# A mixture of 16 experts in two layers: experts written out, tile slots in strict turn, combination products moved, constants issued by SyncE

## The reference

```python
def expert_choice_ffn(h, w_router, w_gate, w_up, w_down):
    b, n, d = h.shape
    cap = max(1, (EC_CAPACITY * n) // N_EXPERTS)
    aff = jax.nn.softmax((h @ w_router).astype(jnp.float32), axis=-1)
    g, idx = lax.top_k(jnp.swapaxes(aff, 1, 2), cap)
    xe = jax.vmap(lambda hb, ib: hb[ib])(h, idx)
    a = jnp.einsum('becd,edf->becf', xe, w_gate)
    up = jnp.einsum('becd,edf->becf', xe, w_up)
    y = jnp.einsum('becf,efd->becd', jax.nn.silu(a) * up, w_down) * g[..., None].astype(h.dtype)
    return jax.vmap(lambda ib, yb: jnp.zeros((n, d), h.dtype).at[ib.reshape(-1)].add(yb.reshape(-1, d)))(idx, y)
```

## Time and profile before

| what | value |
|---|---|
| median of 3 runs | 2744.36 us (2743.35 to 2745.78) |
| the profiled execution's own time | 2746.78 us |
| its span (first to last instruction) | 2745.0 us |
| PE busy | 2536.9 us, 92% |
| DVE busy | 1403.9 us, 51% |
| ACT busy | 1012.0 us, 37% |
| POOL busy | 32.3 us, 1% |
| DMA, mean over the span | 290 GB/s, 796.95 MB |
| granted TensorE clock, mean | 0.991 |

### The profile page before, as it was taken

One profiled execution on the slowest core, in us unless ns is written; L12 is line 12 of the kernel. 1 busy time (PEld: TensorE's weight loads), 2 busy tenths in 40 slices (PEclk: granted clock), 3 DMA queues, 4 the chain that ended last, 5 costly groups with the idle time before them and its releaser, 6 DMA issues.

```text
span 2745.0 us, 33174 instructions
## 1 busy us (share of the span) xinstructions
PE 2536.9 (92%) x12537; PEld 1678.3 (61%) x12537; DVE 1403.9 (51%) x2437; ACT 1012.0 (37%) x1890; POOL 32.3 (1%) x45
## 2 busy tenths in 40 slices
PE   8999997777899999877789999999999999999999
PEld 5666432222465553322237788877888988887887
DVE  4988200001276530000124788668887468975776
ACT  5224111001121421000004656566565456655544
POOL 0000000000000000000000000000000000000000
PEclk9999999999999999999999999999999999999999
DMA  8767799999965369999994487616866418863242
GB/s 353 316 286 278 332 380 426 427 426 428 426 253 240 154 251 426 427 425 427 427 425 204 179 338 279 250 62 253 328 259 275 184 71 327 312 249 127 95 188 100
DMA packets 65268, 796.95 MB, mean 290 GB/s; under 512 B 9276, under 2 KB 10556, under 8 KB 15484
## 3 DMA queue, kind: packets, MB, share of 16 engines
q1 hardware_dynamic: 61424, 790.65, 70.3%
q10 hardware_dynamic: 3724, 4.66, 0.5%
HBM read 794.23 MB, written 1.05 MB: 290 GB/s over the span
## 4 chain that ended last, share of the span: by engine, by line
PE 70%; DMA 19%; DVE 7%; ACT 2%; issue 2%; SPq 0%; ACTq 0%; DVEq 0%
PE banks L2305 12%; PE banks L2316 9%; PE banks L1682 7%; DMA ring<-in_t_up 6%; DMA ring<-in_t_down 6%; PE banks L994 6%; DMA ring<-in_t_gate 6%; PE banks L1007 5%; PE banks L1702 5%; PE banks L2318 4%; PE banks L1761 3%; PE banks L1904 1%; PE banks L749 1%; PE banks L2028 1%; PE banks L871 1%
## 5 line engine op out<-in xcount | busy, mean ns | idle before, releaser
L1682 PE MATMUL banks<-ring,arena 128*64 128x512 f32 x1904 | 432.4, 600 | 84.5 <-DMA ring<-in_t_gate 45.3
L3054 DVE TENSOR_TENSOR arena<-arena,banks 128x512 f32<-128x512 f32 x32 | 22.0, 687 | 757.2 <-PE banks L1682 757.2
L2316 PE MATMUL banks<-u_pair,w_hi 128*128 128x512 f32 x1024 | 362.8, 399 | 1.7 <-DVE u_pair L1284 1.7
L3601 DVE TENSOR_TENSOR ring_lo<-ring,w_hi 128x1024 fp32r<-128x1024 f32 x256 | 311.8, 1220 | 99.1 <-ACT w_hi L2816 97.3
L1682 PEld LDWEIGHTS banks<-ring,arena 128*64 128x64 f32 x1904 | 138.9, 137 | 364.6 <-issue 263.3
L2816 ACT CAST w_hi<-ring 128x1024 fp32r<-128x1024 f32 x256 | 267.6, 1050 | 197.0 <-PE banks L2305 139.9
L2318 PE MATMUL banks<-u_pair,ring_lo 128*128 128x256 f32 x1024 | 287.6, 281 | 0.0
L2465 ACT COPY arena<-banks 32x512 f32<-32x512 f32 (+1 forms) x96 | 55.3, 576 | 499.1 <-PE banks L1702 498.2
L1702 PE MATMUL banks<-ring,arena 128*64 128x512 f32 x896 | 206.1, 608 | 28.3 <-DVE arena L3056 10.5
L2316 PEld LDWEIGHTS banks<-u_pair,w_hi 128*128 128x128 f32 x1024 | 192.4, 188 | 51.3 <-ACT arena L1254 3.7
L2305 PE MATMUL banks<-w_hi,ffn_h_hi 128*128 128x512 f32 x512 | 199.4, 389 | 0.0
(11 more groups left out here) (420 smaller groups left out, 4162.9 us busy)
## 6 DMA issues: line engine op xcount, KB each, us to landing
ring<-in_t_ffn SPq DMA_DIRECT2D x64, 2048.0 KB, 8.1
ring<-in_t_gate SPq DMA_DIRECT2D x60, 2048.0 KB, 29.4
ring<-in_t_ada_dots SPq DMA_DIRECT2D x54, 2048.0 KB, 9.7
ring<-in_t_down SPq DMA_DIRECT2D x48, 2048.0 KB, 28.6
ring<-in_t_up SPq DMA_DIRECT2D x43, 2048.0 KB, 30.3
ring<-in_t_ada SPq DMA_DIRECT2D x18, 2048.0 KB, 17.1
ring<-in_t_up SPq DMA_DIRECT2D x32, 1024.0 KB, 28.5
ring<-in_t_ret_in SPq DMA_DIRECT2D x12, 2048.0 KB, 8.0
```

Of the source, the lines that this page charges most:

```text
L1682: mm = nc.tensor.matmul(PS[64 * h:64 * h + 64, f.bank, :], x, wview(u, 4)[:, k % 4, h * 512:(h + 1) * 512], start=(k == 0), stop=(k == KC ...
L2316: nc.tensor.matmul(PS[:, f.bank, :], hi[:, q, :], u_pair[:, q].rearrange("p s t -> p (s t)"), start=(q == 0), stop=False, skip_group_check ...
L3601: TT(w_lo, w, w_hi[:, n % 4].bitcast(F32), ALU.subtract).then_inc(S("ffn_w_lo"), 1)
```

## The change

- **Experts written out.** All 16 experts stand in the programs of PE, DVE and SP; ACT keeps its loop. All 96 tiles of a layer are one list, and only the last expert's up and second down tiles are sent in pieces.
- **Strict turn.** Tile n takes slot n mod 7 in layer 0 (after the one tile in the arena) and n mod 9 in layer 1.
- **No copies.** PE reads `moe_xe` for all experts. In layer 1 the 64 rows are the tokens of two neighbouring experts, of which ACT copies the right 32. POOL's part (`moe_pool`) goes, `x_cur` with it.
- **`moe_lo` on DVE**, two rows after every second one-hot selection (L3026 of before). In the first set PE multiplies the high parts of all eight chunks before the low ones; the second set keeps groups of four.
- **Banks.** Experts 4 to 15 use banks 0 to 3 only. The combination's first set uses 4 to 7, the second 0 to 3.
- **Combination earlier.** DVE weighs quarters 0 and 1 after experts 9 and 10, quarter 2 after expert 12, quarter 3 after expert 15. PE puts the first set's products of quarters 0, 1, 2 in front of the gate and up tiles of experts 10, 11 and 13.
- **Constants.** SP issues the four loads for the long convolution, after the fourth tile of `dot_units` and a wait for the last combination bank; ACT no longer does.

The diff, cut to its core:

```diff
-            order = [n % n_slots for n in range(24 - 24 % n_slots)]
-            order += [n + (2 if n_slots == RING else 1) for n in range(24 % n_slots)]
...
+            units = [(SLOT, (lambda it, e=e, w=w, h=h: w[e, h])) for e in range(E)
+                     for w in (a["t_gate"][l], a["t_up"][l], a["t_down"][l]) for h in range(2)]
+            at, sent, cleared = [slots[n % n_slots] for n in range(96)], None, plan["cd_out"][-1] if l else plan["ab_out"][-1]
             if l == 0:
-                early = early[0:8] + [RING] + early[8:21] + [slots[2], slots[3]]
-                sent = list(range(7)) + [8, 7] + list(range(9, 24))
+                at = at[0:8] + [RING] + at[8:95]
+                sent = list(range(7)) + [8, 7] + list(range(9, 96))
...
-            fs = fills(p + "experts", [0, 1, 2, 3, 4, 5, 6, 7] * 2, 3, first=1)
+            fs = fills(p + "experts", [0, 1, 2, 3] * 4, 3, first=1)
...
-            for some, it in ((u0, 0), (us, 1)):
-                for n, parts in ((20, 2), (21, 2), (23, 4)):
...
+            for n, parts in ((2, 2), (3, 2), (5, 4)):
+                u = us[6 * (E - 1) + n]
...
-            fills(p + "combine", [0, 1, 2, 3, 4, 5, 6, 7][:4 * ns])
+            fills(p + "combine", [4, 5, 6, 7, 0, 1, 2, 3][:4 * ns])
...
-            load_dots(0, 5)
+            load_dots(0, 4)
+            plan["hy_const_behind"] = dot_units[3]
+            load_dots(4, 5)
...
+            def hyena_constants():
+
+                plan["moe0_combine"][-1].full.wait(sp)
+                sp.dma_start(hy_const, a["k_hyena"]).then_inc(S("hy_const"), 16)
+                sp.dma_start(hf_w1[0:33, :], a["hf_w1"][0]).then_inc(S("hy_const"), 16)
...
-                        for k0 in (0, 4):
+                        span = KC if half == 0 and s == 0 else 4
+                        for k0 in range(0, KC, span):
...
+                def expert_pe(e):
+
+                    beside = {10: 0, 11: 1, 13: 2}.get(e)
+                    if beside is not None:
+                        pe.wait_ge(S("y_lo"), 8 * l + ns * beside + 1)
...
-                                x = x_cur[:, b, k, :]
+                            x = moe_xe[l][:, e // 8, k, cs].rearrange("p e s c -> p (e s c)")
...
-                with pe.Fori(1, 3) as it:
-                    for j in range(4):
-                        expert_pe(j, it)
...
-                expert_pe(3, 3, beside=early)
+                for e in range(E):
+                    expert_pe(e)
+                    if 1 <= e <= ns:
+                        gather(1, [e - 1])
...
-                plan["moe0_combine"][-1].full.wait(act)
-                act.dma_start(hy_const, a["k_hyena"]).then_inc(S("hy_const"), 16)
...
-                    if t == 3:
-                        for r in (2, 3):
+                    if t % 2:
+                        for r in (t - 1, t):
                             dve.wait_ge(S("moe_hi"), 4 * l + r + 1)
                             TT(moe_lo[l][:, r, :], moe_utok[l][:, r, :], moe_hi[:, r, :].bitcast(F32), ALU.subtract)\
-                                .then_inc(S("moe_lo_late"), 1)
+                                .then_inc(S("moe_lo"), 1)
...
-                with dve.Fori(1, 3) as it:
-                    for j in range(4):
-                        expert_dve(j, it)
+                for j in range(4):
+                    expert_dve(j, 1)
+                for j in range(4):
+                    expert_dve(j, 2)
+                    if 1 <= j <= 2:
+                        weigh(j - 1)
                 for j in range(4):
                     expert_dve(j, 3)
-                    weigh(j)
+                    if j in (0, 3):
+                        weigh(2 + j // 3)
...
-            def moe_pool(l, ns):
```

More of the change, by code:

```diff
@@ L397, in load @@
             for s, (width, src) in zip(slots, sources):
-                got.append(Unit(s, landed[s], slot_uses[s] + seen[s] - first * per[s], per[s] if rounds > 1 else 0,
-                                width, src))
+                got.append(Unit(s, landed[s], slot_uses[s] + seen[s], per[s] if rounds > 1 else 0, width, src))
                 seen[s] += 1
@@ L402, in load @@
                 slot_uses[s] += per[s] * rounds
-            stream.append((rounds, looped, first, [got[n] for n in sent] if sent else got))
+            stream.append((rounds, looped, [got[n] for n in sent] if sent else got))
             return got
@@ L1481, in _ @@
                     if looped:
-                        with sp.Fori(first + 1, first + rounds) as it:
+                        with sp.Fori(1, rounds) as it:
                             later(it)
                     else:
-                        for it in range(first + 1, first + rounds):
+                        for it in range(1, rounds):
                             later(it)
                     for s, u in last.items():
-                        users[s] = (u.used, first + rounds - 1)
+                        users[s] = (u.used, rounds - 1)
             for n, (half, t) in enumerate(BY_TOKENS):
@@ L1610, in gather @@
                             pe.wait_ge(S("moe_sel"), 4 * l + 2 * s + 2)
-                        for k0 in (0, 4):
+                        span = KC if half == 0 and s == 0 else 4
+                        for k0 in range(0, KC, span):
                             for low in (0, 1):
-                                if half == 0 and k0 == 0 and not low:
-                                    pe.wait_ge(S("moe_hi"), 4 * l + 2 * s + 2)
-                                elif half == 0 and k0 == 0:
-                                    pe.wait_ge(S("moe_lo_late" if s else "moe_lo"), 2 if s else 2 * l + 2)
+                                if half == 0 and k0 == 0:
+                                    pe.wait_ge(S("moe_lo" if low else "moe_hi"), 4 * l + 2 * s + 2)
                                 src = moe_lo[l] if low else moe_hi
-                                for k in range(k0, k0 + 4):
+                                for k in range(k0, k0 + span):
                                     f = plan[p + f"gather1_{s}"][k // 2] if half else plan[p + "gather0"][4 * s + k // 2]
@@ L1671, in expert_pe @@
                             if beside is not None and k % 4 == 0:
[L1672 removed]
+                                combine(0, h0 + k // 4, (beside,))
                             landed_part(u, k % 4, it)
[L1674 to L1680 removed]
+                            if e == 0 and h0 == 0 and k % 2 == 0:
+                                for s in range(ns):
+                                    plan[p + "gather0"][4 * s + k // 2].free.wait(pe)
+                            x = moe_xe[l][:, e // 8, k, cs].rearrange("p e s c -> p (e s c)")
                             for h in range(2):
@@ L1687, in expert_pe @@
                         mm.then_inc(f.full.sem, 1)
[L1688 removed]
+                        if e == 0 and h0 == 0:
                             for t in range(0, TC * ns, TC):
```

120 lines of the change are left out of this document (35 added, 85 removed).

## The result

The median of the kernel after is 2724.52 us (four runs, 2720.64 to 2725.47) against 2745.02 us for the kernel before in the same session (four runs): a ratio of 0.9923, with an interval from 0.9906 to 0.9941. A second measurement in a later session gave 2726.39 us (five runs) beside 2744.68 us, 0.9931 (0.9918 to 0.9945). The profiled execution took 2725.47 us for a span of 2723.7 us. The forecast was 2724.9.

A forecast was written before the change was run, and what follows sets the result against it. Weight traffic was taken to bound both expert stages. Layer 0: 7.6 + 3.8 + 2.6 + 0.7 - 2.0 = 12.7; layer 1: 2.2 + 4.6 = 6.8; together 19.5 us, giving a median of 2724.9 us, range 2718 to 2732.5.

The forecast's parts named there:

- Strict turn: Layer 0, 350 to 390 us: strict slot order closes a hole in the weight stream, 7.6 us; layer 1, 0.
- The late issue of tile 23: Layer 0: SP issues tile 23 only at 368.17 us, read as waiting for a slot; rival PE's gathering starves rings, 0.06.
- `moe_lo`: Expert selection: moving POOL's subtractions to DVE starts the experts 3.8 us sooner in layer 0, 2.2 in layer 1.
- the two ends 0.55 us behind POOL's: Selections: DVE's scan ends 0.55 and 0.54 us after POOL, so POOL holds DVE; rival, scan slow by itself, chance 0.10.
- this clock in its range: Layer 0, 272.5 to 288.5 us: granted clock 0.89 may rise to 1.0, 1.8 us in each layer, only in the range.
- The tail: End of the last expert: without combination products PE ends sooner after the last landing, 2.6 us layer 0, 4.6 layer 1.
- a rival with whole experts at the low level: Expert stages: idling drops TensorE's clock to 0.50, 14.4 us lost per expert; one per layer gives 2753.7 us; chance 0.04.
- PE's wait for ACT's square: After layer 0's experts: with ACT's four issues gone, PE's 0.73 us wait goes; 0.7 taken, up to 2.1.
- The wait for the constants: hf_mlp's first product after layer 0: constants on SP land last behind four tiles, a new stall, 2.0 us taken.
- The 3.9 that the forecast allowed for: hf_mlp's product: upper bound of the stall on the constants if the small loads trail; 1.6 otherwise.
- Banks, copies, written out: Expert stages: four banks, no POOL copies and straight code each forecast at 0 us.
- The packets of written-out code: Expert streams: rival that about 12 instruction packets per layer for 7 cost 3 us per layer, 2730.9 us; chance 0.10.

The follow-up runs named there:

- run 2: Kernel after with the old order of slots (tiles 21 to 23 in slots 2, 3, 4 in layer 0); 2731.01 us, 0.9953 of the kernel before.
- Run 1: Kernel before with only POOL's moe_lo subtractions given to DVE; 2738.04 us beside 2743.78, ratio 0.9982.
- run 8: Kernel before with only the loops over experts 4 to 11 replaced by straight code on PE, DVE and SP; 2744.06 us beside 2743.91, 1.0005.
- run 3: Kernel after with the combination products of quarters 0 to 2 back in front of expert 15; 2726.41 us, 0.9936 of the kernel before.
- run 4: Kernel after with seven products of zeros in each layer's last expert, ahead of its down product; 2724.12 us, 0.9925 of the kernel before.
- run 5: Kernel after with the last expert's first down tile also waited for in four parts; 2724.27 us, 0.9931 of the kernel before.
- Run 6: Kernel after with both down tiles in parts and the constants issued by ACT as before; 2723.4 us, 0.9926 of the kernel before.

## Why the prediction was right

**Strict turn, right.** Forecast 7.6 us; stream 0 is 7.4 shorter in the two profiles, and run 2 gives some 7 without its late last piece. The late issue of tile 23 was a slot's.

**`moe_lo`, right in mechanism; the agreement by layer is partly luck.** Forecast 3.8 and 2.2 us. Run 1 alone gave 23.87 - 20.02 = 3.85 us and 17.83 - 15.56 = 2.27 us against the profile of before, but 4.9 and 0.8 against run 8. What the two ends 0.55 us behind POOL's had said is confirmed by taking POOL away; the scan's own time is 0.68 and not 0.55. DVE itself saves 4.0 us in layer 0 and 2.1 in layer 1. Two things did not stand in the sum: in run 1 PE waits 1.05 us for `moe_lo`, which only the kernel after covers, and behind PE's pauses of 4.50 and 2.25 us the granted clock fell in three of four cases (profiles of before and of run 8), while it read 1.00 where the pauses were gone. The forecast had this clock in its range, as up to 1.8 us in each layer, but not in its sum. The 3.2 us of selection 1 in the kernel after are partly the earlier high products and partly this clock, which in the kernel before read 0.70 and 0.76 (997 to 1003 us) and in run 8 1.00.

**The tail, wrong in size.** The step that failed reads "Without them PE ends a quarter tile (0.9) plus 0.2 of reaction after the landing", 2.6 + 4.6 us. What the runs showed in its place, as PE's end behind the last landing:

| | layer 0 | layer 1 |
|---|---|---|
| combination in front of expert 15 (run 3) | 4.2 | 4.2 |
| kernel after, clock fallen | 3.8 | 3.8 |
| kernel after, clock held (second profile, layer 0) | 2.2 | - |
| products of zeros (run 4) | 2.2 | 2.2 |
| both down tiles in parts (run 5) | 1.2 | 1.1 |

Two causes, then. About 1 us is geometry: PE starts on the first down tile when it has landed whole (in the kernel after at 682.7 + 30.7 = 713.4 us) and needs 7.1 us from there, to 720.6, while the second has landed at 718.5: 2.1 us behind. The 0.9 holds for a PE that has caught up, and here it can't have. Another 1.7 us is the clock: without the combination products PE pauses 1.64 us ahead of the down product, and the clock then fell in four of six such cases in the profiles of this kernel and of run 2. The forecast had put this as a rival with whole experts at the low level, a gain lost; it came as one product per layer. In layer 1 the 4.6 also started from a disturbed row, 5.7 in place of 4.2.

**ACT and the constants, right in kind, hidden in the result.** PE's wait for ACT's square went as forecast, 0.9 us for 0.7. The wait for the constants, forecast at 2.0, is 0 and 0.40 us in the two profiles of the kernel after, 1.00, 1.34 and 2.39 in runs 4, 5 and 2, whose tails are 2.2, 1.2 and 1.1. The 3.9 that the forecast allowed for has no row behind it and came in no run. A late PE and a late constant lie side by side; removing one shows the other. Run 6 agrees with the Trainium skill (DMA: Bandwidth & Descriptors, Issuing engines are not separate DMA queues): issued by ACT, the constants overtake a tile issued before them, which lands 5.5 us later, and the wait is gone.

**Banks, copies, written out: nothing lost, as forecast.** No run changed the banks or the copies alone; that they cost nothing is read from streams that got no longer. Stream 1 even shortened by 0.8 us, of which no run tells the source. The packets of written-out code cost at most about 1 us a layer (run 8 against run 1), not three.

**The sum.** 19.5 us were forecast and the two measurements gave 20.5 and 18.3. Part of that agreement is luck: the tails fell short by 5.5 us and strict turn by 0.2, while the bridge gave 0.9 more than forecast, since the wait for the constants didn't appear, the selections 1.4, where the clock of the profile of before helped, and stream 1 0.8. That leaves 19.5 - 5.7 + 3.1 = 16.9; the rest of the profiles' 21.3 lies outside the change. With run 8 in place of the profile of before, or the second profile of the kernel after, the same pieces give between 16.0 and 19.4. The medians can't settle 17 against 19.5.

## What to carry to other kernels

When the end of a stage is computed from its last transfer, count from the last transfer at which the engine can still be behind, not from the last of all: two tiles that take 7.1 us of PE and land 5 us apart end 2 us behind the second. Work moved out of the final stretch leaves a pause there, and the pause can cost nearly what the work did (here 1.7 us by the clock, for the 2.0 us between tails of 4.2 and 2.2), so look at what runs right behind it and fill the pause or cut the transfer into pieces. A row that carries a term should be read in a second profile if there is one, since a clock that happened to fall in it (tail 1, 5.7 us for 4.2) goes straight into the forecast.

## What was not expected of the hardware

The granted clock fell or held behind the same pause in the same code. Behind 1.64 to 1.67 us ahead of the last down product it fell four times of six, and always in layer 1 (three profiles). Behind the pause of 2.28 us ahead of the third group it fell in four of eleven profiles (15.36 to 16.86 us for 14.08), and behind the pauses of 4.50 and 2.25 us ahead of the gathers in three cases of four. What decides was not found; products of zeros or transfers in pieces, which leave no such pause, had their product at 7.1 and 14.1 us, the times at full clock, in each profile that has them.

POOL's subtractions held DVE's TENSOR_SCALAR and scan, but not the MAX8 beside them: 0.42 us with POOL and without.
